# A decoder layer with a 32-expert mixture: 32x32 turns on VectorE, 2 MB weight pieces, gather ahead of scatter

## The reference: what is computed

```python
hn = rms_norm(h, norm2_gain)
logits = hn @ w_router + b_router
top_logit, top_idx = lax.top_k(logits, 4)
gate = jax.nn.softmax(top_logit, axis=-1)
# for each expert e and each token routed to it:
hb = x @ w_up[e] + b_up[e]                    # 1024 -> 2048, 8 MB of weights
h_glu, h_lin = jnp.split(hb, 2, axis=-1)
h_glu = jnp.minimum(h_glu, 7.0); h_lin = jnp.clip(h_lin, -7.0, 7.0)
act = h_glu * jax.nn.sigmoid(1.702 * h_glu) * (h_lin + 1.0)
y = (act @ w_down[e] + b_down[e]) * gate      # 1024 -> 1024, 4 MB of weights
```

## Time and profile before

| what | value |
|---|---|
| timed runs, median of 3 | 1487.44 us (1485.11 to 1487.77) |
| profiled execution, span | 1483.1 us |
| PE busy | 1251.7 us (84%) |
| DVE, ACT, POOL busy | 454.0, 202.6, 267.1 us |
| DMA moved | 454.88 MB, mean 307 GB/s |
| first matmul of an expert | 334.21 us |
| last matmuls of an expert | start 1454.27, end 1460.3 us |

### The profile page before, as it was taken

How to read it: one execution, slowest core, us unless ns; L and a number is a source line. 1 busy time by engine, 2 the same in 40 slices (tenths; PEclk the granted TensorE clock), 3 DMA queues, 4 the chain that set the end, 5 groups by cost and what they waited for, 6 DMA issues and landing times.

```text
span 1483.1 us, 29480 instructions
## 1 busy us (share of the span) xinstructions
PE 1251.7 (84%) x11352; PEld 512.8 (35%) x11353; DVE 454.0 (31%) x1105; ACT 202.6 (14%) x299; POOL 267.1 (18%) x391
## 2 busy tenths in 40 slices
PE   6999999968898998899998887979798977996552
PEld 5445555443333333333332332323233322331111
DVE  2451363352322333333332322322232322331112
ACT  2113321011111111111110101101110111110001
POOL 1000011001222222222222121212122211221002
PEclk8999999979999999999999998989999999997766
DMA  9230006458998999969999999999999999999996
GB/s 339 78 113 1 0 1 263 186 214 306 341 326 326 355 361 358 347 243 369 371 344 360 383 385 373 375 330 362 383 388 394 393 365 401 388 361 387 403 377 218
DMA packets 101888, 454.88 MB, mean 307 GB/s; under 512 B 12044, under 2 KB 23240, under 8 KB 69096
## 3 DMA queue, kind: packets, MB, share of 16 engines
q1 hardware_dynamic: 83560, 432.99, 75.1%
q0 software_dynamic: 15120, 20.85, 6.5%
q10 hardware_dynamic: 3184, 0.71, 0.2%
HBM read 437.73 MB, written 16.78 MB: 306 GB/s over the span
## 4 chain that ended last, share of the span: by engine, by line
DMA 55%; PE 26%; issue 8%; SPq 4%; DVE 4%; POOL 1%; POOLq 0%; ACT 0%; DVEq 0%; ACTq 0%
DMA W<-in_w_up_dram 36%; PE B L1066 11%; DMA W<-in_w_down_dram 9%; DMA misc<-hsrow,idx_g 9%; PE B L1309 4%; PE B L1177 4%; PE B L1293 3%; SPq L286 1%; POOL idx_g L487 1%; SPq L374 1%; SPq L291 1%; PE B L1088 1%; PE B L1270 1%; SPq L376 1%; DVE misc L1000 1%
## 5 line engine op out<-in xcount | busy, mean ns | idle before, releaser
L1293 PE MATMUL B<-W,misc 128*32 128x512 f32 x4992 | 606.9, 620 | 107.0 <-DMA W<-in_w_up_dram 83.2
L1309 PE MATMUL B<-W,misc 128*32 128x256 f32 x4992 | 314.8, 395 | 5.0 <-DMA W<-in_w_down_dram 5.0
L1293 PEld LDWEIGHTS B<-W,misc 128*32 128x32 f32 x4992 | 152.0, 111 | 453.4 <-issue 444.5
L499 POOL DMA_INDIRECT hres<-misc,idx_s x78 | 124.8, 1600 | 568.2 <-DVE misc L1002 549.7
L1309 PEld LDWEIGHTS B<-W,misc 128*32 128x32 f32 x4992 | 162.2, 114 | 158.0 <-issue 82.9
L1066 PE MATMUL B<-W 128*128 128x512 f32 x384 | 172.1, 606 | 0.0
L645 ACT ACTIVATE misc<-misc 128x256 f32<-128x256 f32 x78 | 32.5, 417 | 986.7 <-DVE misc L987 986.7
L985 DVE TENSOR_TENSOR misc<-B,misc 128x512 f32<-128x512 f32 x78 | 53.9, 691 | 284.8 <-PE B L1293 284.8
L1066 PEld LDWEIGHTS B<-W 128*128 128x128 f32 x384 | 73.7, 195 | 87.7 <-issue 87.7
L645 ACT ACT_TABLE_LOAD x78 | 100.1, 1283 | 4.4 <-DVE idx_tab L966 3.0
L490 POOL DMA_INDIRECT misc<-hsrow,idx_g x79 | 79.0, 1000 | 59.9 <-POOL idx_g L487 59.9
(11 more groups left out here) (244 smaller groups left out, 604.6 us busy)
## 6 DMA issues: line engine op xcount, KB each, us to landing
W<-in_w_up_dram SPq DMA_DIRECT2D x256, 1024.0 KB, 6.0
W<-in_w_down_dram SPq DMA_DIRECT2D x128, 1024.0 KB, 5.6
W<-in_w_in_dram SPq DMA_DIRECT2D x6, 2048.0 KB, 21.2
W<-in_x_dram SPq DMA_DIRECT2D x8, 512.0 KB, 5.3
W<-in_w_out_dram SPq DMA_DIRECT2D x1, 4096.0 KB, 13.1
hres<-W SPq DMA_DIRECT2D x4, 512.0 KB, 5.1
hsrow<-W SPq DMA_DIRECT2D x4, 512.0 KB, 6.4
W<-hres SPq DMA_DIRECT2D x4, 512.0 KB, 5.3
```

The source lines that it names most:

```text
L499: pool.indirect_dma_start(out=hres, out_offset=bass.IndirectOffsetOnAxis(ap=idx_s[:, 0:1], axis=0), in_=ysb, in_offset=None, compute_op=AL ...
L1293: ins = mm(B[0][BT * j:BT * (j + 1), :].rearrange("p (g h c) -> p g h c", g=2, h=2), xT[:, o:o + BT], up(par)[:, k, :, :, P * j:P * (j + 1 ...
L1309: ins = mm(B[5][BT * j:BT * (j + 1), 0:QC], aT[:, P * h + BT * q:P * h + BT * (q + 1)], down(par)[:, H * h + q, QC * j:QC * (j + 1)], star ...
```

## The change

It has four parts.

1. **Turns on VectorE.** The transposes on PE (L1270, L1277) and the copies out of PSUM (L1012, L1007) go. DVE transposes `xg` to `xT` and the activation to `aT` in 32x32 blocks (`STREAM_TRANSPOSE`, 128x256). For that the rows in `hsrow` are laid out in another order of columns and already hold the norm's gain: `second_norm` becomes 8 strided instructions of 128x128 for each chunk, with a row of gains `n2row` loaded for it (512 KB).
2. **Weights in 2 MB pieces.** An expert is 4 up pieces and 2 down pieces. A partition holds 2 (up) or 4 (down) whole consecutive rows of the matrix, one run of 16 KB in HBM. Still at most two pieces are under way in the loop. Each has its own release (`m_u` 0 to 3, `m_yh`, `m_y`), PE waits for down pieces one by one, and the two biases have semaphores and shuffles of their own.
3. **Gather ahead of scatter.** POOL gathers as soon as DVE has turned a block (`m_xT`), then scatters, then waits for the scatter.
4. **First loads.** 14 MB are loaded before the router's last result, 6 MB more as soon as the rows are in HBM without a wait for POOL, and 4 MB after the gate table.

```diff
+        def load_piece(eng, par, n, e):
+            to = W[par][:, PIECE * n:PIECE * (n + 1)]
+            if n < 4:
+                src = w_up[0, e].rearrange("e (m p r) n -> (e p) m (r n)", m=4, p=P)[:, n]
+            else:
+                src = w_down[0, e].rearrange("e (m p r) n -> (e p) m (r n)", m=2, p=P)[:, n - 4]
+            eng.dma_start(to, src).then_inc(s_w[par][n], 16)
...
-            sp.wait_ge(m_ig, 2)
-            rest = [(0, 2, 0), (0, 2, 1), (1, 0, 0), (1, 0, 1), (1, 1, 0), (1, 1, 1), (1, 1, 2)]
+            first(0, 4)
+            first(1, 0)
+            first(1, 1)
+            sp.wait_ge(s_gtab, 1)
+            sp.wait_ge(s_trash, 32)
+            first(1, 2)
+            first(1, 3)
...
-            scatter(0)
-            with pool.Fori(2, total) as g:
-                pool.wait_ge(m_xp, g + 1)
+            with pool.Fori(3, total + 1) as g:
+                pool.wait_ge(m_xT, g)
                 pool.nop(nofuse=True)
-                gather(g + 1)
-                pool.wait_ge(m_sc, 16 * (g - 1))
+                gather(g)
+                scatter(g - 3)
+                pool.wait_ge(m_sc, 16 * (g - 2))
...
-                V.tensor_scalar(HS[:, c % 2, :], xres[:, c, :], st[:, 40 + c:41 + c], None, ALU.mult).then_inc(s_hs, 1)
+                for m in range(4):
+                    for r in range(2):
+                        ins = V.scalar_tensor_tensor(by_group(HS[:, c % 2, :], m, r), by_row(xres[:, c, :], m, r),
+                                                     st[:, 40 + c:41 + c], by_row(n2row, m, r), ALU.mult, ALU.mult)
...
-                V.tensor_tensor(lin, lin, sg, ALU.mult).then_inc(m_act, 1)
-                x_evac(g + 1)
+                V.tensor_tensor(glu.rearrange("p (m r i) -> p m i r", m=2, r=4),
+                                lin.rearrange("p (m i r) -> p m i r", m=2, r=4),
+                                sg.rearrange("p (m i r) -> p m i r", m=2, r=4), ALU.mult).then_inc(m_act, 1)
+                x_turn(g + 1)
...
+            def act_turn(g):
+                dve.wait_ge(m_act, g + 1)
+                V.transpose(aT, z[:, 0:256]).then_inc(m_aT, 1)
+            def x_turn(g):
+                dve.wait_ge(m_xg, 16 * g + 16)
+                V.transpose(xT, xg).then_inc(m_xT, 1)
...
-                for part in range(NPART):
-                    pe.wait_ge(s_w[par][2][part], loaded)
+                    if loaded is not None and q % 4 == 0:
+                        pe.wait_ge(s_w[par][4 + q // 4], loaded)
```

More of the change, by code:

```diff
@@ L327, in _, with first @@
                 sp.dma_start(xres[:, c, :], x[0, P * c:P * (c + 1), :]).then_inc(s_xres, 16)
[L328 to L333, removed]
+            def first(par, n):
+                load_piece(sp, par, n, slice(par, par + 1))
+            first(0, 0)
+            first(0, 1)
             sp.wait_ge(s_p, NT * H)
@@ L344, in _ @@
                     sp.wait_ge(s_hTe, 2 * NT)
-                    load_parts(0, 2, (2, 3))
+                    first(0, 5)
                 if c == NT - 1:
                     sp.wait_ge(s_out, 2 * NT)
-                    load_parts(0, 1, (0, 1))
+                    first(0, 2)
                     sp.wait_ge(s_bz, 1)
-                    load_bias(sp, 0, slice(0, 1))
-                    load_bias(sp, 1, slice(1, 2))
+                    for par in range(2):
+                        load_bias_up(sp, par, slice(par, par + 1))
+                        load_bias_dn(sp, par, slice(par, par + 1))
                 sp.wait_ge(s_hs, c + 1)
@@ L356, in _ @@
                     .then_inc(s_rowst[c], 16)
-            load_parts(0, 1, (2, 3))
+            first(0, 3)
             sp.wait_ge(s_lge, NT)
-            load_parts(1, 2, (2, 3))
+            first(1, 5)
             for c in range(NT):
                 sp.wait_ge(s_rowst[c], 32)
-            sp.wait_ge(m_ig, 2)
-            rest = [(0, 2, 0), (0, 2, 1), (1, 0, 0), (1, 0, 1), (1, 1, 0), (1, 1, 1), (1, 1, 2)]
[L364 to L371, removed]
+            first(0, 4)
[5 more added lines that the diff above has]
+            first(1, 3)
             with sp.Fori(1, NE // 2) as i:
@@ L1295, in block_up, with block_down @@
                                  start=(k == 0), stop=(k == NK - 1))
-                    if k % 4 == 3:
-                        ins.then_inc(m_u[k // 4], 1)
-            def block_down(g, par, loaded, more):
+                    if k % 2 == 1:
+                        ins.then_inc(m_u[k // 2], 1)
+            def block_down(g, par, loaded):
                 pe.wait_ge(m_aT, g)
-                for part in range(NPART):
-                    pe.wait_ge(s_w[par][2][part], loaded)
-                for h in range(2):
-                    if h == 1 and more:
-                        transpose_block(g + 1)
-                    for q in range(H):
-                        for j in range(H):
-                            ins = mm(B[5][BT * j:BT * (j + 1), 0:QC], aT[:, P * h + BT * q:P * h + BT * (q + 1)],
-                                     down(par)[:, H * h + q, QC * j:QC * (j + 1)],
-                                     start=(h == 0 and q == 0), stop=(h == 1 and q == H - 1))
-                ins.then_inc(m_y, 1)
+                for q in range(NK):
+                    if loaded is not None and q % 4 == 0:
+                        pe.wait_ge(s_w[par][4 + q // 4], loaded)
+                        pe.nop(nofuse=True)
+                    for j in range(H):
+                        ins = mm(B[5][BT * j:BT * (j + 1), 0:QC], aT[:, BT * q:BT * (q + 1)],
+                                 down(par)[:, q, QC * j:QC * (j + 1)], start=(q == 0), stop=(q == NK - 1))
+                    if q % 4 == 3:
+                        ins.then_inc(m_yh if q == 3 else m_y, 1)
@@ L1318, in expert @@
                 if lead:
[L1319 to L1321 removed]
+                    block_down(first, 1 - par, 16 * i + 16 * par)
                 with pe.If_lt(pe.to_reg(first + 1), pe.to_reg(last)):
```

145 lines of the change are left out of this document (63 added, 82 removed).

## The result

The changed kernel takes 1517.9 us (median of 4 runs, 1515.4 to 1520.7) where the kernel before takes 1486.9 beside it: ratio 1.021, 95% interval 1.017 to 1.025. It is slower by 31 us; 1441 was forecast. The profiled execution spans 1513.4 us. Some executions of a kernel come out more than 1.5% above its fastest, and the ratios here leave those out.

A forecast was written before the change was run, and what follows sets the result against it. PE's blocks with their gather wait paced the first 27 blocks, the weight stream the other 51. From 1483 us, -31 +5 -15 +0 -3 = -44 gave a span of 1439, a time of 1443, named 1441; range 1416 to 1469.

The forecast's parts named there:

- the third of the block: POOL's scatter wait at the loop's end: POOL free at 12.7 us, next turn at 14.5, so hidden by 1.8.
- The 7.6 us: Time from the scatter's issue at 450.82 until POOL went on at 458.45, used to put POOL free at 12.7.
- Rival 3: Gather and scatter up to 5 us longer beside 16 KB runs: time 1461 us; 0.20 together with rivals 2, 5.
- Rival 5: Gather misses its turn because POOL's scatter wait outlasts 14.5 us; rival 3's time; 0.20 together with rivals 2, 3.
- Rival 4: Stage B and expert starts: 2 MB pieces with 16 KB runs stream slower, 350 GB/s gives 1517 us; chance 0.08.
- rival 1: Stage B: the stream fills up entirely, 396 GB/s, -37 us in place of -15, time 1421 us; chance 0.15.
- rival 2: Queue was the limit: Stage B gains nothing, Stage A closes only idle share, 1468 us; 0.20 with rivals 3, 5.
- Stage A: Up to 684.7 us, 27 blocks: a block paced by PE takes 11.7 us instead of 12.98; -31 us.
- Stage B: From 684.7 to 1454.2 us, 51 blocks, weight stream: two 2 MB pieces in flight gain 2%, -15 us.
- Run length: Weight stream: 16 KB runs change nothing, 0 us; bounds -1% to +3% (+8 to -23 us in Stage B).
- The start: First blocks and chunk norms: later first turn and eight norm instructions cost +5 us (bounds +2 to +9).
- the end: Last down product: its first half runs while the last piece comes, -3 us.

The follow-up runs named there:

- New order with shallow queue: Changed kernel with 8 KB runs and the scatter's wait moved after the gather, but 2 MB in flight by half pieces: 1483.6 us, ratio 0.991.
- Old order with deep queue: Kernel before the change, with four of its own 1 MB pieces in flight instead of two: 1488.3 us, ratio 1.007.

## Why the prediction was wrong

- **The step that failed** is the third of the block: "POOL is free at 12.7; the next turn is at 14.5. Hidden by 1.8 us." It followed the scatter's wait only to the gather and to x. But `m_is`, which the order after the change shows at L492 and L488, comes after that wait as well, and DVE's `block_out` stands on it ahead of the activation's turn. A block goes from scatter to scatter in 10.9 + 4.5 us, 15.46 in the median, instead of 11.7. I had moved a wait past an index copy and not asked who waits for that copy. The gain of moving it back is 109 us with 16 KB runs and 48 us with 8 KB (1422.1 to 1374.5). Whether a second buffer beside `ysb` would have opened the loop as well was not tried.
- **The 7.6 us** in that step came from one block under the old traffic. Counted in the same way, the median was 7.0 before and is 11.5 now, so POOL is free at 5.1 + 11.5 = 16.6, past the turn at 14.5, and the wait is not hidden even on the path that I had drawn. But that path is not what cost the time: with 8 KB runs the wait lasts 9.0 us, 5.1 + 9.0 = 14.1 lies ahead of the turn, and moving the wait still brought 48 us. Rival 3 had the longer scatter ("up to 5 us more"; measured +4.5) but with a path that goes round once in three blocks. The loop is closed over one block, so all of it comes back in each; it named the right mechanism and the wrong path, and so had 1461. Rival 5 named the threshold (9.4 us from the scatter's issue; measured 11.5) and also took too short a path behind it. Its sign of being wrong, POOL's index copy waiting past DVE's turn, is in the timeline: 720.30 against 712.86 us. So is the other, a later stretch at 377 GB/s or below: 372.
- **Rival 4** names the time that came out, 1517, for a wrong reason. That the time fits it is luck. Its stream at 350 GB/s from 16 KB runs did not come: undisturbed slices show 410 to 421, and 407 GB/s over 690 to 1300 us once the wait is moved.
- **Rivals 1 and 2** spoke of the stream alone. The ceiling lies above the 396 GB/s of rival 1 (410 over 610 us), and the queue is not the limit of A, as rival 2 had it: with the loop open A runs at 391 GB/s instead of 331.
- **Stage A**, -31: +15.2 measured. The engine terms in it were right or better: a turn takes 0.43 to 0.44 us (0.42 forecast), and the PE block without its transposes is 7.08 + 3.45 = 10.5, not 11.66: the 0.56 at the loop's head is gone too, and both products run some tenths faster uncut. One reading in it is off by 0.2 us, which changes nothing: the up product of the earlier trace rows ends at 451.83 + 5.36 = 457.19 and not at 457.0. With the wait moved and 8 KB runs, A takes 290 us from the first to the 28th activation, 57 less than before.
- **Stage B**, -15: +12.7 measured, through the holes at experts of several blocks. The term itself was too small: depth lifts the stream not by 2% but by 4% in the kernel before (375 to 390 GB/s, a third of it in 4 KB runs) and by 10% in the new order with 8 KB runs (372 to 410). I had read the share of 0.99 as nearly full, and 396 as the ceiling; both were those of a queue 2 MB deep.
- **Run length**, 0: right for the stream from 8 to 16 KB. With the wait moved the median of the forty slices is 416 GB/s with 16 KB and 412 with 8 KB, about 1%, inside the bounds, and the highest slice of all, 427, has 8 KB runs. What the term left out is what 16 KB cost the scatter, 2.5 us of each. And the row it stood on misled: "4 to 8 KB showed no loss", but 4 KB runs cost up to 9% of the stream at 4 MB depth (374 and 375 against 410). The earlier trace rows could not show that, since its 4 KB stretch was 4.5 us long. The change also took the down pieces from 4 to 16 KB, so part of the deeper stream's gain may be this.
- **The start**, +5: +6.2 measured, and **the end**, -3: -3.8. Both sizes were right, in part by luck. The first up product begins at 337.90, 3.7 us later than before, as forecast in kind (the eight norm instructions took 2.19 us, forecast 2.8). The other 2.5 us were not in the sum: that product takes 9.56 instead of 7.07 us at a granted clock of 0.74 on average instead of 1.00, after PE had stood idle for 3.44 us until the turn. At the end the last down product does begin before the last weights are there, but only by 0.9 us (1484.85 against 1485.7), not by a half; it takes 3.66 instead of 6.04 us at a granted clock of 1.00, where before it was 0.59 on average, after 4.14 us of idle time. Those 2.4 us were not in the sum either.
- The strided multiply L1004 of the activation, which I did not price, takes 617 ns where its plain form took 0.42 us: 0.2 us a block under cover of the down product.

The change thus held two gains, turns off PE and a deeper stream, that need each other. New order with shallow queue: 0.99 of before. Old order with deep queue: 1.007. Together, without the closed loop: 0.925. The three are not a clean square: the first has PE wait by half pieces, and the second keeps 4 KB runs for its down pieces.

## What to carry to other kernels

When a wait moves on one engine's queue, list every signal that is given behind it and go down each of them, into the queues of the other engines too: the one that binds may be a buffer's release and not the data's arrival. Price a small transfer by the packets that will run beside it and not by its old duration. And a DMA share near 1 does not say that the rate is at its ceiling: try one more piece in flight, and look at what the longer queue does to the small transfers.

## What the runs showed of the hardware

- A scatter of 128 rows of 1 KB beside the weight stream lands in 10.9 us with 16 KB packets, in 8.4 with 8 KB (medians, 4 MB in flight), and in 4.1 where it meets little of the stream. The Trainium skill, "DMA: Bandwidth & Descriptors", section Queues, rings and completion order, says that an engine goes round its queues a packet at a time. These numbers are in line with that; no row shows the turns.
- One core read its weights at 410 GB/s over 610 us with 8 KB runs, and slices of 15 us reached 427 with 8 KB and 421 with 16 KB; with two 1 MB pieces in flight it was 372 to 375 at a share of 0.99 to 1.00. 6 MB in flight brought nothing over 4 MB.
- 4 KB runs brought that down to 374 to 375 at the same depth, whether in DMAs of 512 KB or of 1 MB, in profiled runs that were longer than usual; 6% is the estimate for the usual ones.
- DMAs on 64 of the 128 partitions in alternation: 235 GB/s, 572 ns for a packet of 8 KB instead of 309, in a run of 2135 us; one run in four took 1613.
- The turn of 128x256 float32 in 32x32 blocks on VectorE: 0.43 to 0.44 us; the copy that it replaced took 0.42.
- A DVE multiply of 128x256 float32 that reads and writes 2x32x4 with permuted strides: 617 ns instead of 424.
